# Sine tables at half size, POOL's arithmetic moved to DVE and ACT, and another order of the first part of a hybrid S5 and attention layer

## Chip, cores, metric

One Trainium2 chip, eight cores; each core computes one of the eight sequences of the batch, and no core waits for another. The metric is the device time of the slowest core in microseconds, over several runs. Engines are named as in the profile: PE (TensorE), DVE (VectorE), ACT (ScalarE), POOL (GpSimd), SP (SyncE, which here only issues DMAs).

## What is computed

One decoder layer on x (8, 4096, 1024). A state-space mixer (32 groups of 16 channels, 64 complex states each) and a dilated-window attention (12 heads of 64; dilations 1, 4, 16) run on the same input, are gated, merged and normalised; a squared-ReLU MLP follows.

```python
z = h @ w_in[l]
q, k, v, u, g = jnp.split(z, SPLITS, axis=-1)
...
_, _, h_re, h_im = lax.associative_scan(combine, (a_re, a_im, x_re, x_im), axis=1)
y = (jnp.einsum('blgp,ghp->blgh', h_re, c_re.astype(f32))
     - jnp.einsum('blgp,ghp->blgh', h_im, c_im.astype(f32))
     + d_skip.astype(f32) * ug)
...
mix = (gate_ssm * (y_ssm @ w_ssm_proj[l]) + gate_attn * (y_attn @ w_attn_proj[l])) @ w_out[l]
h = layer_norm(ALPHA * h + mix, ln1_g[l], ln1_b[l])
ff = jnp.square(jax.nn.relu(h @ w_up[l])) @ w_down[l]
h = layer_norm(ALPHA * h + ff, ln2_g[l], ln2_b[l])
```

The diff touches the state-space mixer and what feeds it. The 4096 positions are cut into 256 blocks of 16. Inside a block the recurrence is a matrix product (Toeplitz matrices and packed weights); between blocks it is a scan over 256 columns of a complex state with 64 entries, turned by an angle that grows with the block number. The cosines and sines of these angles are the tables.

## The kernel before

The whole program is a list of operations. Each is added to a named stream with a priority (`P.at(stream, prio)`), an engine, what it reads and writes, and an estimated cost. `Prog.schedule` then sets the order on each engine by a list schedule: per engine it takes, among the heads of the streams, those that can start within 40 ns of the earliest, and of these the one with the lowest priority number. At run time each engine works strictly in that order; semaphores carry the dependencies. Helpers record every operation, so the profile has few lines: L454 is every DMA, L464 every matmul, L469 every transpose, L476 every ACT function, L494 every two-input elementwise operation, L500 and L501 scalar operations, L504 the fused ones, L510 and L511 copies on ACT and DVE, L810 the scan. Memory is one arena; a tile that lies where an older one lay waits for that one's last use.

The streams of the first part, in the order of the code:

- `const`: small coefficients. `f16p` holds the turn per block of each state and group (128 x 32: 64 states twice).
- `U`: POOL issues the loads of x in eight tiles (`x_tile`, float32 to bf16) and of weights; PE multiplies 512 positions at a time by the weights `wu`; ACT empties PSUM into `us`; SP stores it (`u_scratch`).
- `prep`: coefficients on DVE and ACT, ending with eight 128x512 multiplications (`Xb`, `Yb`). Then a loop over 16 batches of two groups: `outer_pair` makes four outer products (in `outer2` one of each pair on DVE, the other on POOL), DVE subtracts twice, PE transposes in float32 and makes the columns of the Toeplitz matrices, ACT copies, and SP stores the packed weights (three DMAs a batch to `sw_scratch`). At the end 16 matmuls make the Toeplitz blocks in `mst`, which one DMA stores (`mw_scratch`). `mst` lies at `Q1`, where the second set of q, k and v comes to lie.
- `tabs`, priority 3: 16 batches of two groups. POOL multiplies block numbers by turns (`tab_a`, L500), DVE takes off whole turns, ACT takes sines and a square, POOL finishes (`tab_c`, L501), SP stores 512 KB (`tab_scratch`). Three buffers (`gcs`).
- `qkv`, priority 5: six rounds (two pairs of heads by three dilations); q, k, v for 4096 positions. In rounds 3 to 5 every second ACT copy releases one cast of MLP weights from float32 to bf16 in DRAM (`pace`, POOL's queue, 34 in all).
- `att`, priority 0: for each round logits on PE, exponential on ACT, multiplication by the bias on DVE, values on PE, addition on DVE.
- `ssm`, priority -1: 32 groups, four sets of input buffers. `ssm_z` (PE), `ssm_scan` (multiply by the tables, add, scan on DVE; multiply by the tables again on POOL into `vv`), `ssm_y` (PE, ACT copy, two DMAs on ACT's queue to `y_scratch`). There is one `vv` and one bank for each of `ssm_z` and `ssm_y`.

After these come, from about 568 us, the gates, projections and the MLP in eight blocks (`p3` and others).

The softmax here doesn't subtract the row's maximum and nothing guards it: scores larger than these inputs give would overflow.

## Time and profile before

| | us |
|---|---|
| four runs | 2020.57, 2052.22, 2025.10, 2049.15 |
| median | 2037.12 |
| the profiled execution, its time | 2020.57 |
| its span (slowest core, core 3) | 2019.0 |
| spans of the eight cores | 2006.8 to 2019.0 |

The profile is that of the slowest core. "Busy" is the time in which an engine executes; a wait is put down to what ended it. The granted clock is a share of 2.4 GHz, 1.00 being all of it. In a row of the table of stretches the columns are: the stretch, its length, busy time of PE, of its weight loads (PEld), DVE, ACT, POOL, each with the number of instructions in brackets, then the granted clock, the DMA share and GB/s.

### The profile page before, as it was taken

The numbers are of one execution on the slowest core, as the hardware profiler recorded it, in microseconds if no ns is written. First come the engines' busy times: TensorE is split into PE (matmuls) and PEld (weight loads), VectorE is DVE, ScalarE is ACT, GpSimd is POOL, SyncE is SP. The second block draws the span as 40 slices with busy tenths as digits, with TensorE's granted clock in tenths as the row PEclk, the third lists the DMA queues.
The fourth block names the chain that finished last, engine by engine and source line by source line (L and its number), as shares of the span: only waits on it lengthen the run. The fifth ranks groups of instructions, "written<-read, shape, count | busy, mean of one in ns | idle before, by whom it ended". The sixth has DMA issues, their size and how long they took to land.

```text
span 2019.0 us, 31329 instructions; the slowest of 8 cores (2006.8 to 2019.0 us)
## 1 busy us (share of the span) xinstructions
PE 1864.2 (92%) x10468; PEld 920.6 (46%) x10468; DVE 967.7 (48%) x1397; ACT 686.2 (34%) x1046; POOL 305.2 (15%) x330
## 2 busy tenths in 40 slices
PE   5787898889958997999999999999999999999997
PEld 2344555556533443444444444444444444444443
DVE  5296577523424632553553454255355335535534
ACT  4443455456546531133213213322321421332120
POOL 5473221211102110001000100200110020010000
PEclk9899999989988998999999999999999999999998
DMA  9846655799996996463663465456456444633531
GB/s 172 178 165 214 189 162 161 153 162 117 119 235 181 244 239 192 157 250 126 213 251 136 152 209 218 137 203 239 147 173 238 178 162 142 252 136 146 219 118 42
DMA packets 133068, 359.71 MB, mean 178 GB/s; under 512 B 10416, under 2 KB 80944, under 8 KB 106544
## 3 DMA queue, kind: packets, MB, share of 16 engines
q1 hardware_dynamic: 73568, 263.23, 37.5%
q0 software_dynamic: 48336, 83.99, 23.2%
q10 hardware_dynamic: 11008, 10.49, 1.8%
q8 instruction: 88, 1.44, 0.3%
q14 instruction: 68, 0.56, 0.1%
HBM read 348.33 MB, written 74.97 MB: 210 GB/s over the span
## 4 chain that ended last, share of the span: by engine, by line
PE 69%; DMA 9%; DVE 6%; issue 6%; ACT 5%; ACTq 2%; POOL 1%; SPq 0%; another core or an unknown queue 0%; DVEq 0%; POOLq 0%
PE ps L464 68%; DVE arena L504 4%; ACT arena L510 2%; DMA arena<-w_up 2%; ACT arena L476 2%; ACTq L454 2%; DMA ya_scratch<-arena 2%; DMA tab_scratch<-arena 2%; DMA arena<-wb_ap 1%; DMA arena<-x_tile 1%; DVE arena L494 1%; PE ps L469 1%; DMA arena<-x 1%; ACT L476 1%; POOL arena L500 1%
## 5 line engine op out<-in xcount | busy, mean ns | idle before, releaser
L464 PE MATMUL ps<-arena 128*128 128x512 bf16 (+4 forms) x10148 | 1847.8, 343 | 121.2 <-ACT arena L510 23.8
L464 PEld LDWEIGHTS ps<-arena 128*128 128x128 bf16 (+2 forms) x10148 | 905.9, 103 | 1044.0 <-issue 214.2
L476 ACT ACTIVATE arena<-ps 128x512 f32<-128x512 f32 (+2 forms) x384 | 260.4, 680 | 427.8 <-PE ps L464 331.5
L504 DVE SCALAR_TENSOR_TENSOR arena<-arena,ps 128x512 f32<-128x512 f32 (+1 forms) x288 | 191.0, 685 | 437.5 <-PE ps L464 382.5
L504 DVE SCALAR_TENSOR_TENSOR arena<-ps,arena 128x512 bf16<-128x512 f32 x256 | 176.9, 691 | 255.2 <-ACT arena L476 255.2
L494 POOL TENSOR_TENSOR arena<-arena 128x512 bf16<-128x512 f32 (+1 forms) x128 | 165.1, 1294 | 695.0 <-DVE arena L504 533.9
L494 DVE TENSOR_TENSOR arena<-arena 128x1024 bf16<-128x1024 bf16 (+6 forms) x235 | 179.6, 789 | 127.3 <-ACT arena L476 120.7
L504 DVE SCALAR_TENSOR_TENSOR arena<-arena 128x1024 f32<-128x1024 f32 (+2 forms) x163 | 192.1, 1179 | 56.4 <-ACT arena L476 34.2
L476 ACT ACTIVATE arena<-arena 128x512 f32<-128x512 f32 (+6 forms) x186 | 101.1, 546 | 329.0 <-DVE arena L1128 250.4
L510 ACT CAST arena<-ps 128x512 bf16<-128x512 f32 (+1 forms) x217 | 120.8, 568 | 129.5 <-PE ps L464 92.2
L476 ACT ACTIVATE arena<-ps,arena 128x512 f32<-128x512 f32 x128 | 87.4, 687 | 166.9 <-PE ps L464 166.6
L454 POOL DMA_DIRECT2D out<-arena x32 | 17.5, 546 | 653.9 <-DVE arena L504 653.9
L1126 DVE BATCH_NORM_STATS2 arena<-arena 128x6 f32<-128x512 f32 x128 | 88.7, 693 | 11.4 <-DVE arena L504 0.2
L476 ACT ACT_TABLE_LOAD x35 | 44.9, 1283 | 121.0 <-DVE arena L1128 107.3
L510 ACT COPY arena<-ps 128x512 f32<-128x512 f32 (+1 forms) x64 | 51.2, 800 | 48.1 <-PE ps L469 26.4
L510 ACT CAST arena<-arena 128x1024 bf16<-128x1024 f32 x32 | 33.4, 1045 | 99.7 <-DVE arena L504 99.6
L469 PE MATMUL ps<-arena 128*128 128x128 bf16 (+1 forms) x320 | 38.3, 238 | 19.8 <-DVE arena L494 11.2
L469 PEld LDWEIGHTS ps<-arena 128*128 128x128 bf16 (+1 forms) x320 | 28.2, 119 | 40.2 <-issue 39.7
L500 POOL TENSOR_SCALAR arena<-arena 128x256 f32<-128x256 f32 x32 | 39.0, 1220 | 29.7 <-DMA tab_scratch<-arena 27.2
L494 DVE TENSOR_TENSOR arena<-ps,arena 128x512 f32<-128x512 f32 (+1 forms) x33 | 22.8, 690 | 42.0 <-PE ps L464 30.3
L494 DVE TENSOR_TENSOR arena<-arena,ps 128x512 f32<-128x512 f32 x64 | 41.0, 680 | 3.9 <-PE ps L464 3.8
L501 DVE TENSOR_SCALAR arena<-arena 128x512 f32<-128x512 f32 (+2 forms) x19 | 10.5, 552 | 49.3 <-POOL arena L500 48.9
(28 smaller groups left out, 163.6 us busy)
## 6 DMA issues: line engine op xcount, KB each, us to landing
arena<-wb_dn SPq DMA_DIRECT2D x64, 1024.0 KB, 5.8
arena<-wb_up SPq DMA_DIRECT2D x56, 1024.0 KB, 4.9
arena<-wb_gate SPq DMA_DIRECT2D x32, 1024.0 KB, 18.7
arena<-wb_out SPq DMA_DIRECT2D x16, 1024.0 KB, 6.8
arena<-x POOLq DMA_DIRECT2D x32, 512.0 KB, 8.2
out<-arena POOLq DMA_DIRECT2D x32, 512.0 KB, 3.9
arena<-x_tile POOLq DMA_DIRECT2D x8, 1024.0 KB, 46.0
tab_scratch<-arena SPq DMA_DIRECT2D x16, 512.0 KB
```

The lines of the kernel that those rows point to most:

```text
L454: return P.add(eng, lambda e: e.dma_start(out=out, in_=in_), R(*reads), R(*writes), dma=True, pk=pk, svc=nb / run * pk / 16.0)
L464: return P.add("pe", lambda e: e.matmul(out, lhsT, rhs, start=start, stop=stop, **kw), R(*reads), R(*writes), cost=c)
L469: return P.add("pe", lambda e: e.transpose(out, in_, ident), R(*reads), R(*writes), cost=c)
L476: return P.add("act", lambda e: e.activation(out, in_, func, bias=bias, scale=scale), R(*reads), R(*writes), cost=c, aset=ASETS.get(func))
L494: return P.add(eng, lambda e: e.tensor_tensor(out, in0, in1, op), R(*reads), R(*writes), cost=ew_cost(eng, out, [in0, in1], True))
L500: return P.add(eng, lambda e: e.tensor_scalar(out, in0, s1, None, op0), R(*reads), R(*writes), cost=c)
L501: return P.add(eng, lambda e: e.tensor_scalar(out, in0, s1, s2, op0, op1), R(*reads), R(*writes), cost=c)
L504: return P.add("dve", lambda e: e.scalar_tensor_tensor(out, in0, scalar, in1, op0, op1), R(*reads), R(*writes), cost=160.0 + 1.06 * fsize( ...
L510: return P.add("act", lambda e: e.copy(out, in_), R(*reads), R(*writes), cost=c)
L1126: P.add("dve", (lambda hf_: lambda e: e.bn_stats(st6[:, hf_ * 6:hf_ * 6 + 6], xb.ap[:, hf_ * 512:hf_ * 512 + 512]))(hf), R(xb), R(m), cost ...
```

## The change

1. Tables: `f16p` is 128 x 16, with the 64 states of two groups one above the other, so one batch serves four groups; cosine, sine and minus sine are kept for 64 states. Eight batches, two buffers. The first step goes from POOL to ACT (`Copy` with a scale), the square and POOL's last step go (cosine by `Abs` and a shifted sine). Each batch has two stores of 384 KB.
2. `outer2` and the last step of `ssm_scan` use DVE only.
3. `mst` moves off `Q1`; the Toeplitz matrices go into `sw_scratch`, so a group loads weights and matrices in one DMA; the halves of the packed weights are stored in four DMAs of 64 partitions; u is laid out so that a group loads it in one DMA; tables are loaded in two halves.
4. The stores of u go from SP's queue to ACT's; `shf` is loaded with x.
5. Priorities: `tabs` 3 to 0, `ssm` -1 to 0. The planner gets a lock: operations of DVE and POOL that read no PSUM are not planned beside each other; DRAM to DRAM transfers are planned 1.5 times as long, the scan shorter. `SLACK` is zero throughout, and `evs` is only counted.

```diff
+                if op.lock and port > t:
+                    t = port
+                    eff = max(eff, t)
...
+                if op.lock:
+                    port = op.fin
...
-    tabs_d = dram_tmp("tab_scratch", [32, 128, 2, 256], F32)
-    sw_d = dram_tmp("sw_scratch", [32, 128, 896], BF16)
-    mw_d = dram_tmp("mw_scratch", [128, 32, 256], BF16)
+    tabs_d = dram_tmp("tab_scratch", [32, 64, 3, 256], F32)
+    sw_d = dram_tmp("sw_scratch", [32, 128, 1152], BF16)
...
+        if out.tensor.name != "arena" and in_.tensor.name != "arena":
+            pk *= 1.5
...
-            dma("sp", u_d[ft], us[ft % 2].ap, [us[ft % 2]], [u_res.res[ft]])
+            dma("act", u_d[ft], us[ft % 2].ap, [us[ft % 2]], [u_res.res[ft]])
...
-    gcs = [ar.alloc([2, 2, 256], F32) for _ in range(3)]
+    gcs = [ar.alloc([2, 3, 256], F32) for _ in range(2)]
...
-        for dst, tab, vec, eng, rd in ((bigA, tabA, vecA, "dve", readsA), (bigB, tabB, vecB, "pool", readsB)):
+        for dst, tab, vec, rd in ((bigA, tabA, vecA, readsA), (bigB, tabB, vecB, readsB)):
...
-            tt(eng, dst.ap, a, b, ALU.mult, rd, [dst])
+            tt("dve", dst.ap, a, b, ALU.mult, rd, [dst])
...
-        dma("sp", dst[64:128, :, 640:896], st.ap[0:64, :, 384:640], [st.res[1]], sres[1])
-        dma("sp", dst[0:64, :, 640:896], st.ap[64:128, :, 384:640], [st.res[1]], sres[2])
-        dma("sp", dst[:, :, 0:640], st.ap, [st], sres[0])
+        for k in range(2):
+            for hf in range(2):
+                dma("sp", dst[hf * 64:hf * 64 + 64, :, 384 + k * 256:640 + k * 256],
+                    st.ap[(hf ^ k) * 64:(hf ^ k) * 64 + 64, :, 384:640], [st.res[1]], sres[1 + 2 * k + hf])
+        dma("sp", dst[:, :, 0:384], st.ap[:, :, 0:384], [st.res[0]], sres[0])
...
-    ar.seek(Q1, A0)
+    ar.seek(c1.span[0], c32.span[0])
     mst = ar.alloc([32, 2, 8, 16], BF16, nres=16)
...
-    dma("sp", mw_d, mst.ap.rearrange("p g o t h -> p g (o t h)"), [mst], [mw_res])
-
-    P.at("tabs", 3)
+    for j in range(4):
+        dma("sp", sw_d[j * 8:j * 8 + 8].rearrange("g p q -> p g q")[:, :, 896:1152],
+            mst.ap[:, j * 8:j * 8 + 8].rearrange("p g o t h -> p g (o t h)"), [mst], [mw_res.res[j]])
+
+    P.at("tabs", 0)
...
     def tab_a(b):
-        cs_, cos_, sin_ = tab_parts(b)
+        cs_ = gcs[b % 2]
         for j in range(2):
-            ts("pool", sin_[:, j, :], iota, f16p.ap[:, 2 * b + j:2 * b + j + 1], None, ALU.mult, None, [smI, f16p], [cs_])
+            act(cs_.ap[:, j, 1, :], iota, AF.Copy, [smI, f16p], [cs_], scale=f16p.ap[:, 2 * b + j:2 * b + j + 1])
...
-        act(sin_, cos_, AF.Sin, [cs_, sgn2pi], [cs_], scale=sgn2pi.ap[:, 0:1])
-        act(cos_, cos_, AF.Sin, [cs_], [cs_], scale=TWO_PI / 2.0)
-        act(cos_, cos_, AF.Square, [cs_], [cs_])
...
+        act(sin_, nsin, AF.Sin, [cs_], [cs_], scale=TWO_PI)
+        act(cos_, nsin, AF.Abs, [cs_], [cs_])
+        act(nsin, nsin, AF.Sin, [cs_], [cs_], scale=-TWO_PI)
+        act(cos_, cos_, AF.Sin, [cs_], [cs_], scale=-TWO_PI, bias=TWO_PI / 4.0)
...
-    P.at("ssm", -1)
+    P.at("ssm", 0)
...
-        tt("pool", vv.ap[:, :, 1:257], ws.ap[:, None, :].to_broadcast([128, 2, 256]), tb.ap, ALU.mult, [ws, tb], [vv])
+        tt("dve", vv.ap[:, :, 1:257], ws.ap[:, None, :].to_broadcast([128, 2, 256]), tb.ap, ALU.mult, [ws, tb], [vv])
```

The order on the engines, first POOL behind the last loads of x, before the change. Here the 128x256 and 128x2x256 operations are the tables, 128x512 the outer products.

```order
L500 TENSOR_SCALAR arena<-arena 128x256 x2
L501 TENSOR_SCALAR arena<-arena 128x2x256
L454 DMA arena<-shifts 128x384
L494 TENSOR_TENSOR arena<-arena 128x512 x4
L500 TENSOR_SCALAR arena<-arena 128x256
L494 TENSOR_TENSOR arena<-arena 128x512 x4
```

On the same engine and place after the change, from the last loads of x on:

```order
L471 DMA arena<-x_tile 128x8x512 x2
L471 DMA arena<-shifts 128x384
L537 MEMSET arena 128x2
L471 DMA arena<-w_qkv 128x1024 x9
L471 DMA arena<-x_blk 128x4096
```

All tables and outer products have left POOL. Next DVE, before, from the last small coefficients; 128x512 x8 makes `Xb` and `Yb`, and the pair behind it is one table batch, of which twelve follow each other before the first outer product.

```order
L494 TENSOR_TENSOR arena<-arena 128x32 x8
L500 TENSOR_SCALAR arena<-arena 128x512 x2
L494 TENSOR_TENSOR arena<-arena 128x512 x8
L501 TENSOR_SCALAR arena<-arena 128x2x256
L494 TENSOR_TENSOR arena<-arena 128x2x256
```

DVE at the same place after the change:

```order
L511 TENSOR_TENSOR arena<-arena 128x32 x5
L518 TENSOR_SCALAR arena<-arena 128x512 x2
L511 TENSOR_TENSOR arena<-arena 128x512 x9
L519 TENSOR_SCALAR arena<-arena 128x2x256
L511 TENSOR_TENSOR arena<-arena 128x2x256
L511 TENSOR_TENSOR arena<-arena 128x512 x2
L511 TENSOR_TENSOR arena<-arena 128x2x256
L511 TENSOR_TENSOR arena<-arena 128x512 x5
```

The ninth 128x512 is the first outer product; one table batch (the scalar operation and the 128x2x256 behind it) stands before the next, and the later single 128x2x256 is a batch's subtraction into the packed weights. Third, one state-space group on DVE, before: `ps,arena` is its first multiplication, 128x256 the addition, L810 the scan, the 128x1024 and the copies are attention.

```order
L511 COPY arena<-ps 128x16x32 x2
L494 TENSOR_TENSOR arena<-ps,arena 128x512
L494 TENSOR_TENSOR arena<-arena 128x256
L810 SCALAR_TENSOR_TENSOR arena<-arena 128x256
L494 TENSOR_TENSOR arena<-arena 128x1024 x2
```

And after:

```order
L530 COPY arena<-ps 128x16x32 x2
L511 TENSOR_TENSOR arena<-ps,arena 128x512
L511 TENSOR_TENSOR arena<-arena 128x256
L831 SCALAR_TENSOR_TENSOR arena<-arena 128x256
L511 TENSOR_TENSOR arena<-arena 128x2x256
L511 TENSOR_TENSOR arena<-arena 128x1024 x2
```

The 128x2x256 behind the scan is the multiplication that was POOL's. Counted over the whole order, the first matmul of `ssm` on PE was number 816 and is number 891, the last was number 2379 and is number 2218.

## Rows read from the trace of the kernel before

**Rows 1.** Table of stretches (us from the start): length, busy time by engine, clock, DMA.

```profile
14.40:104.20 89.80, 69.40 (x411) 34.98 (x412) 32.09 (x54) 44.81 (x75) 38.08 (x41) 0.87 0.96 183
104.20:178.60 74.40, 61.70 (x429) 37.73 (x427) 72.00 (x69) 32.59 (x65) 53.49 (x44) 1.00 0.57 183
178.60:195.10 16.50, 8.22 (x38) 3.55 (x37) 5.39 (x8) 6.30 (x13) 0.51 (x1) 0.89 0.71 217
195.10:404.00 208.90, 184.43 (x1568) 117.36 (x1568) 131.49 (x191) 102.99 (x154) 48.73 (x44) 0.99 0.65 167
404.00:568.20 164.20, 151.18 (x1441) 96.86 (x1442) 61.52 (x98) 94.49 (x133) 24.22 (x39) 0.97 1.01 136
...
800.00:2019.00 1219.00, 1201.28 (x5712) 547.37 (x5710) 565.24 (x822) 306.95 (x478) 93.73 (x109) 1.00 0.49 176
```

**Rows 2.** Waits, 14.4 to 104.2 us: us in total, times, longest.

```profile
DVE arena L501 <- POOL arena L500: 48.1, 11, 9.8
POOL arena L500 <- DMA tab_scratch<-arena: 27.2, 5, 7.6
...
PE ps L464 <- ACT arena L510: 10.6, 3, 6.1
```

**Rows 3.** Chain that ended last, in order of time: start us, us, what.

```profile
47.01 9.90 DMA tab_scratch<-arena
...
59.73 10.88 DMA tab_scratch<-arena
...
571.32 27.23 DMA arena<-wb_ap
```

**Rows 4.** Timeline of DVE, coefficients: start us, us, what.

```profile
34.62 5.29 DVE L494 TENSOR_TENSOR arena<-arena 128x512 f32<-128x512 f32 x8
```

**Rows 5.** Groups by form, DVE, 104 to 180 us: count, busy us, mean ns, idle before.

```profile
L494 DVE TENSOR_TENSOR arena<-arena 128x512 f32<-128x512 f32 x49 | 57.7, 1228 | 0.2
...
L518 DVE MEMSET arena<- 128x2048 bf16 x1 | 1.8, 1765 | 0.4 <-issue 0.4
```

**Rows 6.** Groups by form, POOL, 104 to 180 us.

```profile
L494 POOL TENSOR_TENSOR arena<-arena 128x512 f32<-128x512 f32 x32 | 42.0, 1329 | 18.0 <-DVE arena L494 17.2 <-ACT arena L510 0.8
```

**Rows 7.** Timeline around the Toeplitz store; in brackets idle time before, and its end.

```profile
186.92 0.34 SPq L454 DMA_DIRECT2D mw_scratch<-arena  x1
...
194.40 1.07 ACT L510 CAST arena<-ps 128x512 bf16<-128x512 f32 x2 [7.61 <-DMA mw_scratch<-arena]
...
198.01 0.69 DVE L494 TENSOR_TENSOR arena<-ps,arena 128x512 f32<-128x512 f32 x1 [11.52 <-DMA arena<-tab_scratch]
```

**Rows 8.** Timeline of one state-space group, DVE and POOL.

```profile
291.73 0.69 DVE L494 TENSOR_TENSOR arena<-ps,arena 128x512 f32<-128x512 f32 x1 [0.42 <-PE ps L464]
...
292.52 0.42 DVE L494 TENSOR_TENSOR arena<-arena 128x256 f32<-128x256 f32 x1
293.12 0.69 DVE L810 TENSOR_TENSOR_SCAN arena<-arena 128x256 f32<-128x256 f32 x1 [0.17 <-DVE arena L494]
...
294.14 1.27 POOL L494 TENSOR_TENSOR arena<-arena 128x512 bf16<-128x512 f32 x1 [4.08 <-DVE arena L810]
...
297.70 0.69 DVE L494 TENSOR_TENSOR arena<-arena 128x1024 bf16<-128x1024 bf16 x1 [1.75 <-ACT arena L476]
...
298.31 0.68 DVE L494 TENSOR_TENSOR arena<-ps,arena 128x512 f32<-128x512 f32 x1
```

**Rows 9.** Timeline of ACT's queue: first and last of 32 pairs of y stores.

```profile
204.59 1.64 ACTq L454 DMA_DIRECT2D y_scratch<-arena  x2
...
407.94 1.42 ACTq L454 DMA_DIRECT2D y_scratch<-arena  x2
```

**Rows 10.** Stores of the packed weights: ns an issue, min/median/max, first and last start.

```profile
L454 SPq DMA_DIRECT2D sw_scratch<-arena x48: 365/580/1384, 110.7 to 178.8; - x48
```

**Rows 11.** Groups by form, ACT, 14.4 to 104.2 us.

```profile
L476 ACT ACTIVATE arena<-arena 128x512 f32<-128x512 f32 x39 | 25.7, 660 | 24.5 <-DVE arena L494 22.6
```

**Rows 12.** Waits, 195.1 to 404 us.

```profile
DVE arena L494 <- ACT arena L476: 27.9, 36, 2.0
```

More of the change, by code:

```diff
@@ L36 @@
     __slots__ = ("eng", "emit", "deps", "dma", "sem", "val", "prev", "used", "seq",
-                 "cost", "aset", "stream", "prio", "fin", "pk", "svc", "t0")
+                 "cost", "aset", "stream", "prio", "fin", "pk", "svc", "t0", "lock")
     _seq = 0
@@ L70, in at, with add @@
         self.stream, self.prio = stream, prio
-    def add(self, eng, emit, reads=(), writes=(), dma=False, cost=100.0, aset=None, pk=0.0, svc=0.0):
+    def add(self, eng, emit, reads=(), writes=(), dma=False, cost=100.0, aset=None, pk=0.0, svc=0.0, lock=False):
         op = Op(eng, emit, dma)
-        op.cost, op.aset, op.pk, op.svc = cost, aset, pk, svc
+        op.cost, op.aset, op.pk, op.svc, op.lock = cost, aset, pk, svc, lock
         op.stream, op.prio = self.stream, self.prio
@@ L494, in tt @@
         return P.add(eng, lambda e: e.tensor_tensor(out, in0, in1, op), R(*reads), R(*writes),
-                     cost=ew_cost(eng, out, [in0, in1], True))
+                     cost=ew_cost(eng, out, [in0, in1], True), lock=not (in_psum(in0) or in_psum(in1)))
     def ts(eng, out, in0, s1, s2, op0, op1, reads, writes):
         c = ew_cost(eng, out, [in0], False)
+        lk = not in_psum(in0)
         if s2 is None:
-            return P.add(eng, lambda e: e.tensor_scalar(out, in0, s1, None, op0), R(*reads), R(*writes), cost=c)
-        return P.add(eng, lambda e: e.tensor_scalar(out, in0, s1, s2, op0, op1), R(*reads), R(*writes), cost=c)
+            return P.add(eng, lambda e: e.tensor_scalar(out, in0, s1, None, op0), R(*reads), R(*writes), cost=c, lock=lk)
+        return P.add(eng, lambda e: e.tensor_scalar(out, in0, s1, s2, op0, op1), R(*reads), R(*writes), cost=c, lock=lk)
     def stt(out, in0, scalar, in1, op0, op1, reads, writes):
         return P.add("dve", lambda e: e.scalar_tensor_tensor(out, in0, scalar, in1, op0, op1),
-                     R(*reads), R(*writes), cost=160.0 + 1.06 * fsize(out))
+                     R(*reads), R(*writes), cost=160.0 + 1.06 * fsize(out),
+                     lock=not (in_psum(in0) or in_psum(in1)))
     def cp(eng, out, in_, reads, writes):
@@ L510, in cp @@
             return P.add("act", lambda e: e.copy(out, in_), R(*reads), R(*writes), cost=c)
-        return P.add(eng, lambda e: e.tensor_copy(out, in_), R(*reads), R(*writes), cost=c)
+        return P.add(eng, lambda e: e.tensor_copy(out, in_), R(*reads), R(*writes), cost=c, lock=not in_psum(in_))
     def recip(out, in_, reads, writes):
@@ L714, in build_program @@
         cp("act", wx[:, :, :, 128:192], src[:, :, :, 0:64], [bk], [st.res[0]])
-        sres = [[sw_res.res[(g0 + j) * 3 + part] for j in range(GB)] for part in range(3)]
+        sres = [[sw_res.res[(g0 + j) * 5 + part] for j in range(GB)] for part in range(5)]
         dst = sw_d[g0:g0 + GB].rearrange("g p q -> p g q")
-        dma("sp", dst[64:128, :, 640:896], st.ap[0:64, :, 384:640], [st.res[1]], sres[1])
-        dma("sp", dst[0:64, :, 640:896], st.ap[64:128, :, 384:640], [st.res[1]], sres[2])
-        dma("sp", dst[:, :, 0:640], st.ap, [st], sres[0])
-    ar.seek(argm.span[0], Xb.span[0])
+        for k in range(2):
[3 more added lines that the diff above has]
+        dma("sp", dst[:, :, 0:384], st.ap[:, :, 0:384], [st.res[0]], sres[0])
+    ar.seek(argm.span[0], c1.span[0])
     colb = [ar.alloc([512], BF16) for _ in range(2)]
-    ar.seek(Q1, A0)
+    ar.seek(c1.span[0], c32.span[0])
     mst = ar.alloc([32, 2, 8, 16], BF16, nres=16)
@@ L771, in build_program @@
+    tab_a(0)
+    for b in range(8):
+        if b < 7:
+            tab_a(b + 1)
+        tab_b(b)
     ar.seek(Q1, A0)
     qkv_set()
-    P.at("ssm", -1)
+    P.at("ssm", 0)
     ar.seek(E0)
     NS = 4
-    tabb = [ar.alloc([2, 256], F32) for _ in range(NS)]
-    swb = [ar.alloc([1152], BF16, nres=2) for _ in range(NS)]
-    ugb = [ar.alloc([2, 256], BF16, nres=2) for _ in range(NS)]
+    tabb = [ar.alloc([2, 256], F32, nres=2) for _ in range(NS)]
+    swb = [ar.alloc([1152], BF16) for _ in range(NS)]
@@ L780, in build_program @@
+    ugb = [ar.alloc([2, 256], BF16) for _ in range(NS)]
     t12 = ar.alloc([2, 256], F32)
```

94 lines of the change are left out of this document (51 added, 43 removed).

## Prediction

> **What bounds the kernel now.** I read the page first, then a table of stretches, then the waits, the chain and the timeline of the stretches that lose time. TensorE (PE) is the busiest engine, so only its idle time can be won. The table shows where that is [rows 1]: after 800 us PE works 1201.28 of 1219.00 us, and nothing the diff touches is there. From 14.4 to 568.2 us it is idle for 20.4 + 12.7 + 8.3 + 24.5 + 13.0 = 79 us, and in the first of these stretches its mean granted clock is 0.87.
>
> That first stretch waits for the sine tables [rows 2]: DVE waits 48.1 us for POOL, POOL waits 27.2 us for a table store to land (three buffers), and PE waits 10.6 us for ACT, which waits in the same ring, to empty PSUM. A store takes about 10 us to land, because x is being loaded meanwhile [rows 3]. POOL takes its instructions in order, and the outer products of the preparation stand behind 13 of the 16 table batches. So they start at 104.2 us, though their inputs were ready when eight DVE multiplications ended at 39.91 (34.62 + 5.29) [rows 4].
>
> From 104.2 to 178.6 us DVE is the bound, 72.00 of 74.40 [rows 1]; beside POOL its multiplications take 1228 ns [rows 5], alone 5.29 / 8 = 0.66 us [rows 4]. Then the Toeplitz matrices are stored, at 186.92. An ACT cast waits 7.61 us for that store, since the second set of q, k, v lies on the same memory; PE waits for the cast, and the first group's multiplication starts at 198.01, after 11.52 us of idle DVE [rows 7].
>
> From 198 to 408 us the 32 state-space groups run one after another beside attention rounds 0 to 2, (407.94 - 204.59) / 31 = 6.56 us each [rows 9], with PE busy 88% [rows 1]. One group is a chain: multiply, add, scan on DVE, a multiplication on POOL, PE, a copy, and the next group's multiply, 298.31 after 291.73 [rows 8]. From 404 to 568 us the DMA share is 1.01 [rows 1]: 34 weight casts are under way.
>
> **The change, step by step.** (a) *Tables and preparation.* POOL loses its arithmetic before the MLP: the tables' first step goes to ACT, their last is gone, and 32 outer multiplications go to DVE. The tables are made for 64 states, in 8 batches in place of 16. The outer products now stand right behind the coefficients on DVE, with four table batches among them (first and second order pieces). DVE's work for this loop: 96 multiplications x 0.66 = 63.4; four batches of two such instructions, 5.3; one memset 1.8 [rows 5]; sum 70.5, against 74.4 before.
>
> What can delay it is new: ACT now holds the wait for the table store, with two buffers in place of three, and behind that wait stand the casts that empty PSUM for PE. A batch's first step waits for the stores of the batch two before it. Until now 512 KB took 9.90 to 10.88 us [rows 3]; now it is two stores of 384 KB. Bounds: 10 us as now, or 10.4 x 1.5 = 15.6 if time goes with bytes. I take 12, nearer to the first, since the tables' bytes fall from 8 to 6 MB in all. With four ACT steps of 0.66 us [rows 11], two short ones and the hand-overs, a batch is then 12 + 4 = 16 us. If the first store is issued near 15 us and the second near 30 (two chains of table and coefficient steps alternate on ACT), the later ones go near 46, 62 and 78. DVE starts its products near 50 (39.9, one table batch more, and the longer ACT sequence) and stands for about 6, 8 and 1 us before batches 4, 5 and 6. The loop ends at 50 + 70.5 + 15 = 135.5; the 16 Toeplitz blocks follow with the 8.3 us they take now (178.6 to 186.9): 144 instead of 187, **43 us earlier**. Without any stall it is 129; with stores of 15.6 us, four trips cost 14 more, 158. PE can follow: x arrives as before, and it transposes while it now waits for ACT.
>
> The rows show that DVE and POOL hinder each other in part: at 1.23 us a DVE multiplication, four make 4.9 us a batch beside POOL's two of 1.33 [rows 5, 6]. The Trainium skill (SBUF — State Buffer, Who interferes with whom) says that a DVE instruction with two SBUF inputs and a GpSimd instruction that reads SBUF block each other wholly. By that rule a batch would have been 4 x 0.66 + 2 x 1.33 = 5.3 us, 85 in all, and the move worth 21 us; by the rows it is worth 74.4 - 70.5 = 4, and the sum stands on the rows.
>
> (b) *Stores and loads of the preparation.* SP issues 80 stores of the packed weights in place of 48. At the median 0.58 us of an issue [rows 10] they take 46 us beside a loop of 85 (50 to 135.5): hidden, with five staging buffers as cover. If that cover went and each issue took the longest seen, 1.38 us, a batch would be 5 x 1.38 = 6.9 us and the loop 110. The matrices no longer lie under the second q, k, v, so ACT's 7.61 us go [rows 7], and PE has round 1 to do in that place; (a) holds that. From the Toeplitz store to the first group it is 11.1 us now (186.92 to 198.01). Four stores of short runs take the place of one, and one load less follows: I take 12, between none (a gain of 8) and twice as long. So the groups start at 156 instead of 198.
>
> The Trainium skill (SBUF — State Buffer, Summary: rules for kernel authors) advises one DMA over all 128 partitions, not several, which speaks against the new halves of 64; that would be paid in SP's time, which the 46 us above hold.
>
> (c) *The group chain.* The last multiplication leaves POOL, where it takes from the scan's end at 293.81 to 295.41, 1.60 us, for DVE: 0.69 like the first one, plus the 0.17 that lies before a scan, 0.86 [rows 8]. That alone gives 6.56 - 0.74 = 5.8 us a group. The floor is DVE's own work: 0.69 + 0.42 + 0.69 + 0.69 = 2.5 and, counted in the new order, 67 attention instructions to 32 groups, 2.1 x 0.69 = 1.45, together 4.0. I take 5.2, nearer to the chain, since other work still stands between the groups in PE's queue. 32 x 5.2 = 166, the end at 322 against 408. But less of the rest is done by then: the last state-space matmul is number 2218 of PE's order, before it was 2379. The 161 that are left cost 161 x 208.9 / 1568 = 21 us [rows 1]. Net, at the same place of the order: **65 us earlier**.
>
> (d) *Rounds 3 to 5 and the MLP.* The casts hang on the same ACT instructions, so they start earlier too. DMA is full there [rows 1], and already now the first MLP stage waits 27.23 us for a weight [rows 3]. With no groups beside them the rounds ask for the casts in less time than DMA needs. I take **10 us given back**, bounds 0 (the groups' own loads are gone from there, too) and 20. From the MLP on the order is the same on all engines.
>
> Sum: 2020.57 - 65 + 10 = **1966 us**, against the profiled execution (span 2019.0, 1.6 us around it). It was the lowest of the four runs; their median is 16.5 above, and the top of the range allows for that.
>
> **Rivals.** *More:* no stall in (a), groups at 4.5 us (144 instead of 166), and DMA keeps up: 15 + 22 + 10 more, which the 79 us of idle PE cap at 2020.6 - 79 = 1942. For it: DVE has few other waits in the new order. Against: PE never ran without idle time beside the groups [rows 1].
>
> *The stores still pace it:* with 20 us to land, a batch is 24 us; batch 6 comes near 117 on DVE, 42 us of the loop and 8 us of blocks follow: 167 instead of 187, 20 earlier. Then (c) at 5.8 wins 24 and leaves 21, nothing is given back: 1998. For it: two buffers, and ACT holds the wait. Against: fewer bytes a store than 20 us would need.
>
> *Slower:* the groups lose their precedence over attention (priority -1 becomes 0), and their last step joins an in-order queue in which DVE already waits up to 2.0 us for an ACT exponential [rows 12]. If each group meets one such wait and one more attention multiplication, 5.8 + 2.0 + 0.7 = 8.5 us, 272 in all, 62 over the 210 now, less the 43: 2040, and with a stall more of the stores past 2060. It decides from 6.56 + 43 / 32 = 7.9 us a group. Against it: the third pair of order pieces has the same two attention instructions a group as before.
>
> *Not what holds PE:* if x and not the ring of tables paces PE to 104 us and the loop ends no earlier, only (c) is left, 24 less 21: 2017. Against: PE's 10.6 us for ACT [rows 2].
>
> **How the numbers follow.** Forecast 0.52, more 0.12, stores 0.20, not what holds PE 0.06, slower 0.10. The range: low without a stall and with 4.5 us a group, 37 less, of which I count 30: 1936. High with 158, 5.8 us and 20 given back: 14 + 19 + 10 more, 2009, and a little for the spread of the runs, 2012. That leaves out most of the slower case and of the last one, and some of "more". About 2%, 40 us, is what a measurement of this kernel can tell from no change. Faster than that, below 1980, are all of "more", nine tenths of the forecast and a little of the stores: 0.62. Slower by over 2% is most of the slower case, 0.07. The rest, 0.31, is within.
>
> **What would show it.** Right: the outer multiplications on DVE from near 50 to near 135 us, at 0.66 us; no ACT wait for the Toeplitz store; y stores 5 to 5.5 us apart, the first near 160; the gain at the first MLP stage the same as at the end. Wrong: ACT waiting over 40 us in total for table stores, y stores over 6 us apart, or a gain at 322 us that is gone by the first MLP matmul, which would name the casts as the bound.

## The result, and the profile after

The changed kernel takes 1987.81 us (median of 10 runs) against 2026.83 for the kernel before (16 runs on the same chip). The ratio is 0.9793, 95% interval 0.9745 to 0.9841: 2.1% or some 42 us less, clear of no change at all; whether it is more than 2% the interval leaves open. The forecast was 1966, its range 1936 to 2012. Ratios leave out runs that were disturbed; where too few were left for one, the undisturbed times stand beside those of the same chip.

The profiled execution of the changed kernel took 1999.93 us. The list of spans and clocks by core:

```profile
core 3: 1970.8 us, clock 0.981
...
core 5: 1998.4 us, clock 0.965
```

Core 5 is the slowest, mostly because of its clock in the first 200 us: of the 28 us that it lies behind core 3, 17 are there at the first group (last section). So I compare core 3 with core 3, as the rows of before are of core 3. First the table of stretches of before, with columns as in [rows 1], in stretches that suit both kernels:

```profile
14.40:75.00 60.60, 49.57 (x296) 24.47 (x296) 25.09 (x42) 27.97 (x46) 23.61 (x24) 0.92 1.10 196
75.00:200.00 125.00, 94.62 (x599) 54.00 (x600) 86.18 (x91) 56.69 (x106) 68.46 (x61) 0.92 0.61 183
200.00:365.00 165.00, 147.18 (x1352) 98.43 (x1351) 106.52 (x155) 83.69 (x122) 37.17 (x32) 1.00 0.59 169
365.00:545.00 180.00, 163.22 (x1387) 97.26 (x1386) 75.57 (x118) 99.50 (x143) 34.48 (x49) 0.97 0.98 137
545.00:800.00 255.00, 208.36 (x1131) 99.02 (x1130) 101.20 (x152) 108.43 (x148) 34.93 (x36) 0.91 0.92 222
```

The same stretches after:

```profile
14.40:75.00 60.60, 42.21 (x249) 23.66 (x250) 26.89 (x47) 27.01 (x44) 0.00 (x0) 0.86 1.10 192
75.00:200.00 125.00, 117.54 (x759) 66.83 (x757) 66.91 (x108) 65.84 (x121) 2.23 (x5) 0.97 0.74 185
200.00:365.00 165.00, 151.46 (x1379) 102.60 (x1377) 122.08 (x199) 80.80 (x121) 5.13 (x9) 0.98 0.74 196
365.00:545.00 180.00, 163.95 (x1501) 101.98 (x1500) 69.21 (x111) 102.48 (x146) 25.42 (x41) 0.95 1.02 131
545.00:800.00 255.00, 231.02 (x1122) 103.66 (x1121) 122.94 (x182) 109.92 (x147) 34.30 (x35) 0.97 0.83 225
```

Length less busy time is PE's idle time: before 11.0, 30.4, 17.8, 16.8 and 46.6 us, after 18.4, 7.5, 13.5, 16.1 and 24.0. That is 122.6 against 79.5, 43 us less, nearly the 48 by which the core's span fell (2019.0 to 1970.8). Two stretches pay: 75 to 200 us (23) and 545 to 800 us (23). The groups' own stretch gives 4, and the first one loses 7. Core 3 is the fastest core of this run. On the six cores whose clock was not lowered (all but 4 and 5), each beside itself before, the five stretches give -7, 22, 4, 2 and 15 us on average, and the spans fell by 26 to 48 us.

The preparation after, timeline of DVE, to be held against [rows 4, 7]:

```profile
50.37 5.89 DVE L511 TENSOR_TENSOR arena<-arena 128x512 f32<-128x512 f32 x9
...
77.13 0.43 DVE L519 TENSOR_SCALAR arena<-arena 128x512 f32<-128x512 f32 x1 [7.34 <-ACT arena L493]
...
144.72 1.29 DVE L511 TENSOR_TENSOR arena<-arena 128x512 f32<-128x512 f32 x2 [2.73 <-PE ps L481]
153.91 0.69 DVE L511 TENSOR_TENSOR arena<-ps,arena 128x512 bf16<-128x512 f32 x1 [7.90 <-PE ps L481]
...
192.14 0.69 DVE L511 TENSOR_TENSOR arena<-ps,arena 128x512 f32<-128x512 f32 x1 [21.81 <-PE ps L481]
```

SP's Toeplitz store and its first load for a group:

```profile
170.78 4.61 SPq L471 DMA_DIRECT2D sw_scratch<-arena  x4
182.51 0.71 SPq L471 DMA_DIRECT2D arena<-u_scratch  x1
```

ACT's queue, first and last pair of y stores [rows 9]:

```profile
196.78 1.65 ACTq L471 DMA_DIRECT2D y_scratch<-arena  x2
...
346.88 1.24 ACTq L471 DMA_DIRECT2D y_scratch<-arena  x2
```

The outer products end at 146.0. After that DVE waits for PE only: for the columns at 153.91, then until the Toeplitz store at 170.78, then 21.81 us until the first group at 192.14. The y stores are (346.88 - 196.78) / 31 = 4.84 us apart, before 6.56. The waits from 14.4 to 104.2 us [rows 2]:

```profile
DVE arena L519 <- ACT arena L493: 34.0, 6, 10.8
...
ACT arena L493 <- DMA tab_scratch<-arena: 18.9, 4, 7.4
...
PE ps L486 <- DVE arena L511: 9.8, 2, 6.8
```

The last line is part of what the first stretch lost: PE stands 6.8 us for the first outer products, which DVE takes behind a batch of tables.

One group after [rows 8]; the last multiplication (first of the x3) follows the scan at once, the next group's first one is at 278.75:

```profile
273.87 0.69 DVE L511 TENSOR_TENSOR arena<-ps,arena 128x512 f32<-128x512 f32 x1 [0.51 <-PE ps L481]
...
275.20 0.69 DVE L831 TENSOR_TENSOR_SCAN arena<-arena 128x256 f32<-128x256 f32 x1
275.99 1.90 DVE L511 TENSOR_TENSOR arena<-arena 128x512 bf16<-128x512 f32 x3
278.75 0.69 DVE L511 TENSOR_TENSOR arena<-ps,arena 128x512 f32<-128x512 f32 x1 [0.86 <-PE ps L481]
```

Last, two marks further on: the first weight cast on POOL's queue and the second load of the GLU weights on SP's, first of before, then of after. The first cast hangs on the same copy in both kernels, behind matmul 2201 of PE's order before and 2233 after, so it is "the same place".

```profile
371.36 0.70 POOL L454 DMA_DIRECT2D wb_glu<-w_glu  x1 [3.08 <-ACT arena L476]
...
604.27 0.32 SPq L454 DMA_DIRECT2D arena<-wb_glu  x1
```

```profile
351.19 0.67 POOL L471 DMA_DIRECT2D wb_glu<-w_glu  x1 [2.58 <-ACT arena L529]
...
570.49 0.32 SPq L471 DMA_DIRECT2D arena<-wb_glu  x1
```

| gain in us (core 3) | predicted | measured |
|---|---|---|
| Toeplitz store, 186.92 to 170.78 | 43 | 16 |
| first group, 198.01 to 192.14 | 42 | 6 |
| last y store, 407.94 to 346.88 | 86 | 61 |
| first cast, 371.36 to 351.19 | 65 | 20 |
| second GLU load, 604.27 to 570.49 | 55 | 34 |
| end, 2019.0 to 1970.8 | 55 | 48 |

On the six cores the first cast gains 15 to 21 us, the second GLU load 21 to 34 and the end 26 to 48, so core 3 stands near the top of each range.

The end came out near the forecast, the way there did not: on core 3, 45 us too much at the first cast, and 28 us behind it (10 to 28 by core) that were not forecast.

### The profile page after: what moved, and what is told of

It reads as the page before. It is cut to its first block, busy times and chain, and to the rows that moved or that the text cites. A ratio compares the mean times of both kernels' runs of the same rounds, so it can differ in the third digit from the quotient of the medians.

```text
span 1998.4 us, 30936 instructions; the slowest of 8 cores (1970.8 to 1998.4 us)
## 1 busy us (share of the span) xinstructions
PE 1881.2 (94%) x10468; PEld 931.9 (47%) x10468; DVE 952.1 (48%) x1444; ACT 689.7 (35%) x1052; POOL 171.8 (9%) x218
## 4 chain that ended last, share of the span: by engine, by line
PE 77%; DMA 6%; DVE 6%; ACT 5%; issue 3%; ACTq 1%; SPq 0%; another core or an unknown queue 0%; DVEq 0%; POOL 0%; POOLq 0%
PE ps L481 76%; DVE arena L522 4%; ACT arena L493 3%; DMA tab_scratch<-arena 2%; DMA arena<-w_up 2%; ACT arena L529 2%; PE ps L486 1%; DMA arena<-wb_gate 1%; ACT L493 1%; DVE arena L511 1%; ACTq L471 1%; DMA ya_scratch<-arena 1%; DMA y_scratch<-arena 0%; DVE arena L1151 0%; SPq L471 0%
## 5 line engine op out<-in xcount | busy, mean ns | idle before, releaser
L481 PEld LDWEIGHTS ps<-arena 128*128 128x128 bf16 (+2 forms) x10148 | 916.1, 104 | 1019.9 <-issue 222.6
L511 DVE TENSOR_TENSOR arena<-arena 128x512 f32<-128x512 f32 (+7 forms) x291 | 171.1, 622 | 127.6 <-ACT arena L493 109.3
L493 ACT ACTIVATE arena<-arena 128x1 f32<-128x1 f32 (+7 forms) x187 | 97.3, 525 | 298.8 <-DVE arena L1153 249.4
L511 POOL TENSOR_TENSOR arena<-arena 128x512 bf16<-128x512 f32 x64 | 81.8, 1278 | 508.7 <-DVE arena L522 508.7
L511 DVE TENSOR_TENSOR arena<-ps,arena 128x512 f32<-128x512 f32 (+1 forms) x33 | 22.8, 690 | 48.4 <-PE ps L481 48.3
L486 PEld LDWEIGHTS ps<-arena 128*128 128x128 bf16 (+1 forms) x320 | 29.9, 124 | 32.3 <-issue 32.3
L533 DVE RECIPROCAL arena<-arena 128x1 f32<-128x1 f32 (+1 forms) x65 | 10.8, 166 | 40.4 <-ACT arena L493 40.0
L471 POOL DMA_DIRECT2D arena<-x x32 | 17.1, 536 | 125.8 <-DMA out<-arena 109.6
```

The lines of the kernel that those rows point to most:

```text
L471: return P.add(eng, lambda e: e.dma_start(out=out, in_=in_), R(*reads), R(*writes), dma=True, pk=pk, svc=nb / run * pk / 16.0)
L481: return P.add("pe", lambda e: e.matmul(out, lhsT, rhs, start=start, stop=stop, **kw), R(*reads), R(*writes), cost=c)
L486: return P.add("pe", lambda e: e.transpose(out, in_, ident), R(*reads), R(*writes), cost=c)
L493: return P.add("act", lambda e: e.activation(out, in_, func, bias=bias, scale=scale), R(*reads), R(*writes), cost=c, aset=ASETS.get(func))
L511: return P.add(eng, lambda e: e.tensor_tensor(out, in0, in1, op), R(*reads), R(*writes), cost=ew_cost(eng, out, [in0, in1], True), lock=no ...
L533: return P.add("dve", lambda e: e.reciprocal(out, in_), R(*reads), R(*writes), cost=160.0 + 6.2 * fsize(out))
```

## Experiments

"Order kept" means: the list schedule is made for the unaltered program, its order on each engine is replayed, and an instruction that changes its engine is put in at its planned time. `var` is true in the program that runs and false in the one that is planned. Where a difference of two ratios is below 0.005 (10 us), the intervals overlap and the verdict rests on the places in the trace.

**Control.** 

> The changed kernel itself, every instruction in the same order, as the measure for the other runs of this chip: 0.974 to 0.984 of the kernel before.

 Measured: 0.9819 (0.9706 to 0.9932), in agreement.

**The step of the groups, in both orders (e1, e5).**

```diff
+        tt("pool" if var else "dve", vv.ap[:, :, 1:257], ...)   # e1, in the changed kernel
+        tt("dve" if var else "pool", vv.ap[:, :, 1:257], ...)   # e5, in the kernel before
```

> The changed kernel with its order kept, but the last multiplication of each group (32 of them) back on POOL. If that step lies on the path of every group, each of the 31 periods grows by the 0.74 us of the prediction, from 4.84 to about 5.6 us: the last y store comes 23 us later, PE's idle time from 200 to 365 us goes from 13.5 to some 36, and the whole is 18 to 25 us longer. If PE, busy 151 of 165 us there, sets the period and the groups' chain has slack, the 0.74 us are covered for the most part: a period under 5.1 us and the whole under 8 us longer.

> The kernel before with its order kept and one part of the change alone: the last multiplication of each group on DVE in place of POOL. If the end follows the groups (the run with that multiplication back on POOL lost 20 us at the last group and as much at the end), the period falls from 6.56 to about 5.8 us, the last y store from 408 to about 385, and the whole is 15 to 23 us shorter. If the loads at the start of the MLP pace the end (the casts then start earlier and DMA is full), the groups end as early, but the second load of the GLU weights stays within 6 us of 604 and the whole is at most 8 us shorter.

First and last y store, the changed kernel with the step on POOL (core 3):

```profile
200.40 1.64 ACTq L507 DMA_DIRECT2D y_scratch<-arena  x2
...
369.75 1.24 ACTq L507 DMA_DIRECT2D y_scratch<-arena  x2
```

The kernel before with the step on DVE (core 3):

```profile
204.65 1.69 ACTq L490 DMA_DIRECT2D y_scratch<-arena  x2
...
404.41 1.27 ACTq L490 DMA_DIRECT2D y_scratch<-arena  x2
```

PE's waits for the step on POOL (us in total, times, longest; core 3), in e1 from 200 to 365 us:

```profile
PE ps L517 <- POOL arena L547: 20.3, 22, 3.3
```

In the kernel before, from 195.1 to 404 us:

```profile
PE ps L464 <- POOL arena L494: 0.2, 1, 0.2
```

In the changed order the step is on the path: PE waits 20.3 us for it, a group takes 5.46 us in place of 4.84, the last y store comes 23 us later (14 to 23 by core), and PE is idle for 25.6 us from 200 to 365 in place of 13.5. The kernel takes 2023.22 us in its one undisturbed run, where 0.9793 of that chip's kernel before would be 2002: some 21 longer. In the old order the step is not on the path: PE waits 0.2 us for it, and with the step on DVE a group takes 6.44 us in place of 6.56, ratio 0.9989 (0.9973 to 1.0004). Neither theory of e5 had this: the groups themselves hardly end earlier.

There PE's order sets the period. From the first of the groups' matmuls to the last it holds 1563 instructions before and 1327 after, 49 and 41 a group; by the 184.43 us in which PE did 1568 matmuls [rows 8], 0.118 us each, 49 are 5.8 of the 6.56 us. This is a count; no run took that other work out between the groups. Of the 61 us at the last y store 38 are there with the step still on POOL (407.94 to 369.75), and the step brings 23.

**Outer products back on POOL (e2).**

```diff
-        for dst, tab, vec, rd in ((bigA, ...), (bigB, tabB, vecB, readsB)):
+        for dst, tab, vec, eng, rd in ((bigA, ..., "dve", readsA), (bigB, tabB, vecB, "pool" if var else "dve", readsB)):
```

> The changed kernel with its order kept, but the second product of each of the 32 pairs of outer products back on POOL. If PE is what bounds 75 to 192 us (it waits only 7 us there), the sharing of work between DVE and POOL is worth little: DVE's multiplications rise from 0.61 to about 1.2 us, half as many, the last outer product within 5 us of 146, the Toeplitz store within 5 us of 171, the whole at most 4 us longer. If this move is what won the 23 us of PE's idle time between 75 and 200 us, the last outer product comes 15 us later or more, the Toeplitz store near 186 as before the change, and the whole is 12 us longer or more.

Groups by form on DVE and on POOL, 50 to 155 us (core 3):

```profile
L547 DVE TENSOR_TENSOR arena<-arena 128x512 f32<-128x512 f32 x58 | 61.8, 1112 | 4.2 <-PE ps L517 3.6
...
L547 POOL TENSOR_TENSOR arena<-arena 128x512 f32<-128x512 f32 x32 | 44.3, 1400 | 88.2 <-DVE arena L547 88.2
```

The last outer product ends at 149.3 (146.0 in the change), the Toeplitz store is issued at 174.2 (170.8). Ratio 0.9825 (0.9782 to 0.9867). DVE stood 19.3 us for tables there instead of 21.0, so the move of the 32 products is worth 3.3 + 1.7 = 5.0 us, where the prediction had 4 by the rows; what counted was that the tables left POOL's queue ahead of them.

In the loop a batch of four products on DVE beside two on POOL takes 4.13 us; if the two blocked each other wholly it would take 4.8, four times 0.66 and twice the 1.06 us of a product on POOL while DVE was idle. So the rule that the prediction weighed (the Trainium skill, SBUF — State Buffer, Who interferes with whom) does not hold in full here: part of the work overlaps. Most of the 21 us that the prediction gave it came from something else: it took POOL's time beside DVE, 1.33 us, which holds the mutual delay already. With 1.06 the same sum gives some 13.

**Three table buffers (e3); less of PE's work (e4).**

```diff
+        gcs.append(ar.alloc([2, 3, 256], F32))                   # e3, in free memory behind us
...
+                       [...]).drop = var and fp == 1 and 0 < kc < 5    # e4, u
+                   [...]).drop = var and rnd == 1 and 0 < kc < 5       # e4, q and k
```

> The changed kernel with its order kept and three table buffers in place of two. DVE's four waits for table batches among the outer products (5.7, 7.3, 4.1 and 3.9 us) should go or halve, so that the last outer product comes near 135 instead of 146. If the ring of tables is what kept the prediction's 43 us from coming, the Toeplitz store moves from 171 to 161 or earlier and the whole is 8 us shorter or more. If PE is what holds it there, the store moves by at most 5 us and the whole by at most 3.

> The changed kernel with its order kept, but with 128 matmuls left out (4 of 8 terms of the sums for the second half of u, 64 matmuls, and for q and k of round 1, 64), 128 x 0.213 = 27 us of PE's work, the first half of it ahead of the Toeplitz blocks, the second between them and the first group. If PE bounds 75 to 192 us, the Toeplitz store comes 10 us earlier or more (171 to 161 or less) and the first group's multiplication 20 us earlier or more (192 to 172 or less); the whole is 22 to 27 us shorter. If tables, outer products and their stores bound it, the Toeplitz store stays within 4 us of 171, the first group comes at 183 or later, PE's idle time between 75 and 200 us grows from 7.5 to over 20, and the whole is at most 14 us shorter.

SP's Toeplitz stores and the first group on DVE, with three buffers (core 3):

```profile
164.90 3.98 SPq L507 DMA_DIRECT2D sw_scratch<-arena  x4
...
186.26 0.69 DVE L547 TENSOR_TENSOR arena<-ps,arena 128x512 f32<-128x512 f32 x1 [21.81 <-PE ps L517]
```

With less work for PE (core 3):

```profile
162.00 4.03 SPq L507 DMA_DIRECT2D sw_scratch<-arena  x4
...
179.23 0.69 DVE L547 TENSOR_TENSOR arena<-ps,arena 128x512 f32<-128x512 f32 x1 [17.68 <-PE ps L517]
```

Its table of stretches, 75 to 200 us:

```profile
75.00:200.00 125.00, 106.71 (x742) 62.66 (x741) 75.95 (x123) 70.59 (x128) 2.76 (x6) 0.95 0.82 210
```

Three buffers move everything from the loop's end to the first group by 6 us (3 to 8 by core); ratio 0.9763 (0.9737 to 0.9788). ACT then waits for no table store, yet DVE still stands 16.4 us for tables, which ACT writes behind casts that wait for PE. Some 27 us less of PE's work move the store by 9 and the first group by 13 (6 to 12 and 9 to 14 by core); PE is then idle for 18.3 us in this stretch (7.5), and the ratio is 0.9755 (0.9728 to 0.9783). So my theory at that point, that PE alone bounds the stretch, falls. But part of the relief went to the clock: PE's granted clock in the stretch was 0.95 here (0.89 on core 0) where it was 0.97. Each relief shows the next limit after 6 to 13 us: the ring of tables, PE, and the way from the Toeplitz store to the first group, which is 17 us (17 to 21 by core) even with PE relieved (162.00 to 179.23).

**The casts and the start of the MLP (e6, e7).**

```diff
+                for c in casts[28:]: c.late = mx                            # e6, in the kernel before
+            after.w = slots[len(casts) + 12 - (8 if var else 0)]            # e7
```

> The kernel before with its order kept, but the last six casts of weights (six of 34, the rest of the down weights) issued behind the first POOL addition of the MLP, near 600 us, instead of from 525 to 554. If the queue of casts, which land 30 to 66 us after their issue there, holds the first loads of the MLP, then the y loads land in about 12 us instead of 24, the 27 us wait for a weight falls under 12, the second load of the GLU weights comes at 592 or earlier instead of 604, and the whole is 10 to 20 us shorter. If these loads take as long by themselves, or the later casts take it back at the up weights, the whole is within 4 us of the kernel before.

> The changed kernel with its order kept, but every cast of weights issued eight places earlier, the first eight in round 2, beside the groups, where the DMA share is 0.74. If DMA paces the start of the MLP (in all runs so far the second load of the GLU weights comes 219 to 226 us after the first cast, whenever the groups end), it comes at 562 or earlier instead of 570, and the whole is 5 to 12 us shorter than the changed kernel. If the casts crowd the groups' own loads, the period rises from 4.84 to over 5.1 and the whole is 3 us longer or more. If neither, the whole is within 3 us of it.

DMA issues from 575 to 700 us (the last number is the median from issue to landing), the kernel before and e6, both core 0:

```profile
arena<-x POOLq DMA_DIRECT2D x8, 512.0 KB, 23.7
```

```profile
arena<-x POOLq DMA_DIRECT2D x8, 512.0 KB, 40.3
```

PE's longest waits from 545 to 800 us, in the same order:

```profile
PE ps L464 <- DMA arena<-wb_gate: 21.0, 1, 21.0
```

```profile
PE ps L500 <- DVE arena L540: 15.2, 5, 10.7
```

The queue of casts does hold the first weights: the 21.0 us wait goes, and the second GLU load comes at 585.45 in place of 605.11 on this core. But the casts then hold up x, which lands in 40.3 us instead of 23.7, and a wait of 15.2 us for the sum with x takes the place. Ratio 0.9998 (0.9989 to 1.0008): one wait for another. With early casts the groups pay: their packed weights land in 12.6 us instead of 4.7 while casts run, the period rises to 5.31, the last y store comes at 363.80, and the ratio is 0.9883 (0.9858 to 0.9908), 18 us worse than the change.

**The order.** e8 is the changed kernel with `P.at("tabs", 3)` and `P.at("ssm", -1)`, planned anew; e9 is e8 with three table buffers.

> The changed kernel, planned anew with the old priorities (tables 3, groups -1). The prediction's slower case rests on the groups having lost their precedence. If the gain is that of the moved work and not of the order, the whole is within 6 us of the changed kernel, the period between 4.6 and 5.1 us. If precedence matters, the groups run at under 4.6 us and the whole is 6 us shorter or more. If the tables need the new priority, the outer products again start near 100 us, the first group comes near 200 and the whole is 12 us longer or more.

> The changed kernel planned anew with the old priorities (tables 3, groups -1) and with three table buffers. With the old priorities alone the groups began near 173 us and ended near 329, 17 us before those of the changed kernel, yet the second load of the GLU weights stayed at 567 to 576, where every run with early groups has it (567 to 573). If that is a floor set by DMA from the first cast on, the earlier groups of this run change nothing: load at 565 or later, whole within 4 us of the changed kernel. If not, an earlier end of the groups passes on: load at 560 or earlier, whole 8 us shorter or more.

In e8 the four Toeplitz stores and the first group (core 3):

```profile
146.66 4.17 SPq L471 DMA_DIRECT2D sw_scratch<-arena  x4
...
176.29 0.69 DVE L511 TENSOR_TENSOR arena<-ps,arena 128x512 f32<-128x512 f32 x1 [5.08 <-PE ps L481]
```

The store comes 24 us before that of the change and near the 144 of the forecast, with two buffers; the first group 16 us before (192.14). The outer products end at 116.2 in place of 146.0. So the two new priorities held the store back by more than the ring (6) or PE's work (9); why so much no run takes apart. The last y store comes at 328 to 337 us by core (347 to 351), but a group takes 4.89 to 5.04 us: precedence moves the groups as a whole and makes none of them faster. And the first cast stays (351 to 360 beside 351 to 356), so does the second GLU load (567 to 577 beside 570 to 579), and the undisturbed time is 1984.09 beside 2025.75 or more for the kernel before: as fast as the change.

In e9 the first cast itself comes earlier, at 334 to 340, the second GLU load at 556 to 563, and the times are 1969.38 and 1969.75; ratio 0.9705 (0.9573 to 0.9836). So the 567 us of e8 were no floor. What holds is the distance from the first cast to that load: 218 to 224 us after the change and in e9, 214 to 220 in e8, 227 to 235 before. The stretches of e9 (core 3) show where the cast's 12 us (351.19 to 339.23) come from:

```profile
14.40:75.00 60.60, 51.80 (x326) 28.83 (x327) 45.34 (x78) 27.83 (x49) 0.00 (x0) 0.94 1.11 194
75.00:200.00 125.00, 116.24 (x770) 65.49 (x768) 65.77 (x106) 72.40 (x124) 2.23 (x5) 0.96 0.81 209
```

PE's idle time in the first stretch is 8.8 us in place of 18.4, 10 of the 12 us; in the second it stays about what it was (8.8, 7.5). In e8, with two buffers, the first stretch has 10.2 to 12.6: the priorities bring most of this, not the third buffer.

**Longer packets (e10).** The weights to be cast lie in rows of 4096 elements in DRAM (`src[i, c]` in place of `src[i, :, c]`).

> The changed kernel with its order kept, but the weights that are cast lie in DRAM so that each cast reads and writes rows of 4096 elements in place of 512 (fewer and longer packets for the same bytes). If DMA's throughput from the first cast on sets the start of the MLP, and the short packets cost it time, the casts land earlier (13 to 31 us now), PE's idle time from 545 to 800 us falls from 24 to under 18, the second load of the GLU weights comes at 565 or earlier, and the whole is 4 to 10 us shorter. If the time goes with bytes, or if the longer packets hold up other loads, the whole is within 3 us, or longer.

DMA issues from 345 to 560 us, of the control and with long rows (both core 4):

```profile
wb_dn<-w_down POOLq DMA_DIRECT2D x16, 512.0 KB, 24.0
```

```profile
wb_dn<-w_down POOLq DMA_DIRECT2D x16, 512.0 KB, 6.6
```

Waits of DVE and PE with long rows, 365 to 545 us:

```profile
DVE arena L558 <- DMA ya_scratch<-arena: 19.8, 2, 12.1
...
PE ps L517 <- ACT arena L529: 19.5, 8, 10.0
```

The down casts land in a quarter of the time, and PE's wait for the gate weights falls from 18.6 to 6.0 us. But the first of these waits is new: DVE's normalisation needs its buffer back and stands up to 12.1 us for the 128 KB store of it; ACT stands behind DVE and PE behind ACT, 19.5 us where the control has 4.3. So PE's idle time only moves: from 545 to 800 us it falls from 35.0 to 17.6, from 365 to 545 it rises from 15.2 to 28.3. Ratio 0.985 (0.9717 to 0.9984): no gain.

**Weights in two steps, on top of e9 (e11).**

```diff
+                gp.append(load_piece("gate", mq + 1, after=[gp[0], wsp_, wap_] if blk == 0 and m == 0 else ()))
```

> The run with old priorities and three table buffers, and in addition the weights of the first gate stage in two steps: the loads of the second to fourth gate piece (and the two output weights behind them on SP) wait until the first gate piece and the two projections have landed. There PE stood 14 to 19 us for the first gate piece, which landed 23 us after its issue, with 8.5 MB of loads issued within 15 us of each other. If these loads hold each other up, it lands in 10 to 15 us, PE's wait falls under 10 us, and the whole is 5 to 10 us shorter than without this step, 0.963 to 0.969 of the kernel before. If it is the casts still in DMA's queues that hold it, the wait stays over 14 us, and the later pieces come later too: the whole is the same as without the step (0.970) or up to 5 us longer.

PE at the first gate piece, whose load SP issued at 525.78 (core 2):

```profile
548.62 0.59 PE L481 MATMUL ps<-arena 128*128 128x512 bf16 x1 [18.25 <-DMA arena<-wb_gate]
```

The piece still lands after 22.8 us: it is not the loads beside it. That leaves the casts in the queues, as e6 showed for the kernel before; no run here took them away from this load. Ratio 0.9713 (0.9693 to 0.9733), no better than e9, but with a narrow interval, all of it below that of the changed kernel (0.9745 to 0.9841): old priorities and a third buffer, with this step, beat both kernels, though on another chip than the change.

## Why the prediction was right and wrong

*(a) Mis-sized: 43 us became 16 at the store and 6 at the first group.* The mechanism held: outer products on DVE from about 55 us, stores of 10.1 to 10.9 us (I took 12), ACT's wait for them 18.9 us. Of the stalls, 21.0 us where I had 15: 13.0 behind the ring's stores, and 8.0, not foreseen, behind ACT's casts that wait for PE. Three terms failed. "PE can follow" failed: from 75 us on PE has no idle time to speak of, and its in-order queue puts matmuls of u and of rounds 0 and 1 between those of the preparation, so the blocks took 146.0 to 170.8, not "the 8.3 us they take now". "I take 12" failed for the way from the store to the first group: it took 21.4 us, and 17 even with PE relieved (e4). PE was busy for all 21.3 us from 170 to 191.3; and the four stores land first (SP's next load is at 182.51), then a group's loads. And the order had no term: the new priorities cost PE 7 us before 75 and, by e8, some 24 at the store (170.78 to 146.66). With the old priorities the 43 us at the store would have come out nearly whole, without the kernel being faster for it.

*(b) Right in part.* ACT's wait for the Toeplitz store is gone and SP's issues are hidden. PE did round 1 in that place: 118 of its matmuls stand between the blocks and the first group, 9 before.

*(c) The step named was not the bound.* "The last multiplication leaves POOL ... that alone gives 5.8 us a group" is refuted by e5; by the counts the period is PE's order, and only in the new order is the chain next (e1). The size, 4.84 for 5.2, was near for another reason. The conversion failed as well: "161 matmuls cost 21 us" left 65 at the same place, where 20 were measured. PE was 89% busy there before and 92% after and did 1379 matmuls from 200 to 365 us against 1352: faster groups mostly changed places with other work. The 65 were all of PE's idle time up to 404 us [rows 1], 20.4 + 12.7 + 8.3 + 24.5 = 65.9; to win them by the groups alone, PE would have had to run without a gap.

*(d) Wrong in sign: 10 given back became 14 gained (5 to 17 on the six cores).* The rounds ask for the casts over the same time (182 us from first to last cast in both), but the groups' loads and stores no longer run beside the first of them: 408 - 371 = 37 us of that traffic before, none after. The median down-weight cast lands in 18.3 us in place of 29.9. The y loads, on which the next stage's GELU waits, land in 12.23 us; before they were issued at 561.46 and ACT began at 585.98. So PE's wait for that stage shrinks, from 545 to 800 us on core 3, first before, then after:

```profile
PE ps L464 <- DVE arena L504: 17.4, 3, 16.7
```

```profile
PE ps L481 <- DVE arena L522: 8.6, 2, 8.1
```

With a wait of 2.8 us for other weights that is gone, these are some 11 of the 23 us that this stretch gives on core 3. That the missing traffic of the groups is the cause is argued, not shown: no run moved that traffic alone. e7 shows the other side of it (early casts slow the groups' loads), e6 that casts delay loads in this stretch. I had named this as the bound of 0 ("the groups' own loads are gone from there, too") and not let it go below. The prediction also listed PE's idle time only up to 568 us and so left out the stretch with most of it, 46.6 us from 545 to 800.

*Rivals.* "The stores still pace it" holds for 6 us (e3), with stores of 10 us and not 20. "Not what holds PE" was right that PE has limits of its own there (in the first stretch it waits 9 us for x in both kernels, which the prediction did not list), but the loop did end 31 us earlier (176.8 to 146.0). "Slower" is out: with the groups' precedence restored a group is no faster and the kernel as fast. That forecast and result agree within 22 us is luck: the errors had both signs: on core 3, 45 us too much up to the first cast and 38 too little behind it (a loss of 10 forecast, a gain of 28 measured).

## What to carry to other kernels

Where one in-order engine is the bound, count its idle time by stretch first: it caps each saving, and a mark on a side chain (the end of the groups) is no gain until the same place in that engine's order moves. A step taken off a chain can be worth nothing while the written order holds the chain apart (e5) and some 20 us once the order is tight (e1), so test it in both orders. A priority that a schedule is planned with has a price as well: plan once with the old ones (e8). A saturated DMA stretch passes a wait on to the next transfer (first weights, x, groups, a small store): moving the same traffic did not help (e6, e7, e10); that less traffic beside it did is the likely reading of (d).

## What the hardware showed unasked

In the profiled run cores 4 and 5 had a granted clock of 0.80 from 14 to 200 us, with PE busy for 165.5 of 186 us on both, and core 3 had 0.94 with 159.8. Core 5 did 918 matmuls in that time, core 3 1006, and its first group came at 208.96, 17 us behind core 3's. From 100 to 120 us, with PE busy all 20 us on each of these cores, cores 4 and 5 had 0.81 and did 130 matmuls each, core 3 had 1.00 and did 174. So 0.81 lies between the two levels of the clock, 1.00 (2.4 GHz) and 0.50 (1.2 GHz), and PE was as busy on these cores as on core 3. In the control run it was cores 2 and 3, at 0.91 from 800 to 1000 us, where cores 0 and 1 had 1.00. Why two neighbouring cores get less is open.

With long rows on one queue a small store on another came late (the 12.1 us above). The Trainium skill (DMA: Bandwidth & Descriptors, Queues, rings and completion order) says that a DMA engine takes turns between queues at packet boundaries; the run agrees in kind; it does not show the order of the packets.
